# Hybrid decoder layer, one core: decay tables behind the softmax maxima, sample rows by transpositions, one-column row selector, row norm ahead of the attention

## What is computed

```python
h = rms_norm(x, norm_g) * (1 + scale) + shift
proj = h @ w_in                        # D_MODEL 1024 -> 3328 columns
qa, ka, va, za, qb, fb, ib, zb = jnp.split(proj, SPLIT_POINTS, axis=-1)
...                                    # A: QK norm, partial rotary
ya = window_attention(qa, k_all, v_all, pos0, sinks) * jax.nn.silu(za)
...                                    # in it: m = maximum(max(s), sink); p = exp(s - m) / sum
log_f = jnp.log(lbh + (1 - lbh) * jax.nn.sigmoid(zf))     # B: decay f ...
k_in = (1 - lbh) * jax.nn.sigmoid(-zf)                    # ... and key k, from fb
o, s_new = hgrn2_chunked(qb, log_f, k_in, ib, s0)         # S <- f S + k v^T, o = q S
yb = rms_norm(o, o_norm_g) * jax.nn.silu(zb)
g_a, g_b = jnp.split(jax.nn.sigmoid(h @ w_merge + b_merge), 2, axis=-1)
y = g_a * (ya @ w_proj_a) + g_b * (yb @ w_proj_b)
out = x + gate * (y @ w_out)
```

## Time and profile before

| | |
|---|---|
| median of 3 runs | 1617.27 us (1616.54 to 1617.92) |
| profiled execution, its own time | 1617.43 us |
| its span, first to last instruction | 1614.5 us |
| busy shares of the span | PE 97%, PEld 79%, DVE 47%, ACT 34%, POOL 51% |
| chain that ended last | PE 88% |
| HBM traffic | 106 GB/s over the span |

### The profile page before, as it was taken

The page is one execution under the profiler, slowest core; times in us unless marked ns, Lnnn a source line. Parts: engine busy times, 40 slices in busy tenths (PEclk is TensorE's granted clock), DMA queues, the critical chain, the costliest instruction groups (busy, mean ns, idle before and its releaser), DMA issues.

```text
span 1614.5 us, 32929 instructions
## 1 busy us (share of the span) xinstructions
PE 1564.4 (97%) x13608; PEld 1268.2 (79%) x13608; DVE 752.2 (47%) x1930; ACT 555.2 (34%) x1131; POOL 822.6 (51%) x1080
## 2 busy tenths in 40 slices
PE   5999999999999999999999999999999999999998
PEld 2787778877888778888879877788888977788886
DVE  3665554233458655532245665623334655623122
ACT  3334323434322432333422343244432344143330
POOL 2425333556673633455756452437777363337671
PEclk9999999999999999999999999999999999999999
DMA  9723112344565321233365331223455331123351
GB/s 321 230 77 93 54 55 66 92 120 129 170 164 124 102 77 51 70 93 117 92 184 132 85 92 54 67 72 115 137 174 156 86 105 54 55 79 91 93 163 67
DMA packets 304971, 175.87 MB, mean 109 GB/s; under 512 B 74158, under 2 KB 290567, under 8 KB 304808
## 3 DMA queue, kind: packets, MB, share of 16 engines
q1 hardware_dynamic: 304824, 173.79, 37.3%
HBM read 159.69 MB, written 11.96 MB: 106 GB/s over the span
## 4 chain that ended last, share of the span: by engine, by line
PE 88%; DVE 6%; issue 2%; ACT 2%; SPq 2%; DMA 1%; POOL 0%; DVEq 0%
PE ps_D L751 50%; PE ps_D L748 24%; PE ps_XD L806 2%; SPq L503 2%; ACT p_or_hf L1107 1%; PE ps_XB L885 1%; PE ps_XA L918 1%; PE ps_XA L907 1%; PE ps_XB L933 1%; PE ps_XA L938 1%; PE ps_XB L932 1%; DMA th_t<-in_w_ada 1%; DVE p_or_hf L1462 1%; PE ps_XC L818 1%; PE ps_XA L885 1%
## 5 line engine op out<-in xcount | busy, mean ns | idle before, releaser
L1650 POOL TENSOR_TENSOR w_lo_t<-w_raw,w_hi_t 128x256 fp32r<-128x256 f32 x928 | 676.9, 764 | 632.1 <-ACT w_hi_t L964 631.8
L751 PE MATMUL ps_D<-h_hi_t,w_hi_t 128*128 128x512 f32 x1024 | 414.9, 405 | 0.1
L751 PE MATMUL ps_D<-h_hi_t,w_lo_t 128*128 128x512 f32 x1024 | 400.4, 391 | 1.2 <-issue 1.2
L751 PE MATMUL ps_D<-h_lo_t,w_hi_t 128*128 128x512 f32 x1024 | 400.8, 391 | 0.0
L964 ACT ACTIVATE w_hi_t<-w_raw 128x1024 fp32r<-128x1024 f32 x232 | 240.2, 1052 | 78.8 <-PE ps_D L748 45.0
L751 PEld LDWEIGHTS ps_D<-h_hi_t,w_hi_t 128*128 128x128 f32 x1024 | 193.0, 188 | 51.9 <-issue 14.8
L751 PEld LDWEIGHTS ps_D<-h_hi_t,w_lo_t 128*128 128x128 f32 x1024 | 192.8, 188 | 42.0
L751 PEld LDWEIGHTS ps_D<-h_lo_t,w_hi_t 128*128 128x128 f32 x1024 | 193.2, 189 | 36.3 <-issue 0.3
L748 PE MATMUL ps_D<-w_hi_t,h_hi_t 128*128 128x384 f32 (+1 forms) x384 | 141.9, 370 | 3.0 <-issue 1.4
L748 PE MATMUL ps_D<-w_hi_t,h_lo_t 128*128 128x384 f32 (+1 forms) x384 | 136.4, 355 | 1.5 <-issue 1.5
L748 PE MATMUL ps_D<-w_lo_t,h_hi_t 128*128 128x384 f32 (+1 forms) x384 | 136.4, 355 | 0.0
(11 more groups left out here) (390 smaller groups left out, 2373.5 us busy)
## 6 DMA issues: line engine op xcount, KB each, us to landing
w_raw<-in_w_in SPq DMA_DIRECT2D x72, 512.0 KB, 3.9
w_raw<-in_w_merge SPq DMA_DIRECT2D x64, 512.0 KB, 4.0
w_raw<-in_w_in SPq DMA_DIRECT2D x64, 256.0 KB, 3.9
w_raw<-in_w_out SPq DMA_DIRECT2D x32, 512.0 KB, 4.1
x_or_AT<-in_x_prompt SPq DMA_DIRECT2D x20, 512.0 KB, 5.2
w_raw<-in_w_proj_a SPq DMA_DIRECT2D x64, 128.0 KB, 3.0
w_raw<-in_w_proj_b SPq DMA_DIRECT2D x32, 256.0 KB, 3.2
xr<-in_x_prompt SPq DMA_DIRECT2D x16, 512.0 KB, 4.8
```

What stands on the lines that cost most here:

```text
L751: ins = mm(bank[:, :], w[:, s0, k0 + k, :], a[:, k, :], start=go, stop=end)
L1650: ins = g_.tensor_tensor(w_lo[:, c, k:k + 2], w_raw[:, n % NRAW, k:k + 2], f32(w_hi[:, c, k:k + 2]), ALU.subtract)
```

## The change

Five edits:

- DVE's evacuation of units f0, f1 and f3 (their two tables) moves behind the side tasks: f0 and f1 to the end of the second half of their own unit, f3 to the end of the first half of the next unit (`AFTER_SCORES`).
- `sx` transposes the four 128x128 pieces of srow as they are (128 columns each), and DVE then adds the four row groups in a new step, `column_sums`, whose result the tanhs of ACT and the products of DVE read. The bank is now freed by DVE in every case, and in the first pass ACT waits for DVE.
- `vB` is one matmul: the values' high and low parts lie stacked in rows 64 to 71 and 96 to 103 of one tile, with zeros between, and the stationary operand is one column of a small selector, broadcast to 128.
- The large selector's cast at the start of the second pass is gone, a second cast of the values' high part takes its place, and three small instructions that fill the new tiles stand at DVE's start.
- `srms` moves from unit 26 to unit 10 of the second pass and `soss` from unit 28 to unit 11.

```diff
@@ -208,8 +208,8 @@
         for _b in range(NS):
-        put(1, 26, 1, "srms", 0)
-        put(1, 28, 1, "soss", 0, "XC")
+        put(1, 10, 1, "srms", 0)
+        put(1, 11, 1, "soss", 0, "XC")
...
+AFTER_SCORES = {UIX[("f", 0)]: (UIX[("f", 0)], 1), UIX[("f", 1)]: (UIX[("f", 1)], 1), UIX[("f", 3)]: (UIX[("f", 3)] + 1, 0)}
+SUMMED = {a: n + 1 for n, a in enumerate((2, 3, 6, 7, 8, 9, 10))}
...
-        rowsR = sb("rows_r", [8, 1280], F32R)
+        rowsR = sb("rows_r", [104, 1280], F32R)
-        esel = esel_t[0:8, :].rearrange("p (b n) -> p b n", b=NS)
-        ib_hi, ib_lo = rowsR[:, 0:512], rowsR[:, 768:1280]
+        ib_hi, ib2 = rowsR[0:8, 0:512], rowsR[64:104, 0:512]
...
+        esel = sb("esel", [P, NS], F32R)
...
+        red = part(64).rearrange("p (s c b) -> p s c b", s=2, b=NS)
...
                     else:
                         for c in range(nb):
-                            ins = mm(bank[:, NS * c:NS * c + NS], srow[:, P * c:P * c + P], sel[:, 0:NS],
-                                     start=True, stop=True)
+                            ins = tr(bank[:, P * c:P * c + P], srow[:, P * c:P * c + P], ident[:, :])
...
                 elif task == "vB":
                     s.wait_ge("s_ib", 1)
-                    mm(bank[:, :], esel[:, a, :], ib_hi, start=True, stop=False)
-                    ins = mm(bank[:, :], esel[:, a, :], ib_lo, start=False, stop=True)
+                    ins = mm(bank[:, :], esel[64:104, a:a + 1].broadcast_to([40, P]), ib2, start=True, stop=True)
...
                 elif task == "sOT":
-                    s.freed(1, "sx", 4 + a)
+                    s.wait_ge("s_oT", a + 1)
                     for c in range(4):
                         ins = tr(bank[0:NS, P * c:P * c + P], oT[:, 4 * a + c, :], ident[:, :])
...
                 elif task == "sx" and it == 0 and a != 4:
-                    s.full(*key)
-                    src = bank[:, 0:32].rearrange("p (h b) -> p h b", b=NS)
+                    s.freed(*key)
+                    src = red[:, SUMMED[a] % 2]
                     if a == 3:
-                        s.free(fn(thS, src, ACT.Tanh, scale=0.5), *key)
+                        s.done(fn(thS, src, ACT.Tanh, scale=0.5), "s_th")
                     elif a < 7:
                         s.done(fn(tS[:, 0:4] if a == 2 else tS[:, 4:8], src, ACT.Tanh, scale=0.5), "s_th")
                     else:
                         for c in range(4):
                             kind, j = BLOCKS[GROUPS[0][a][c]]
                             cb = 8 * (kind == "gb") + j
-                            ins = fn(thg[:, 2 * j + (kind == "gb"), :], bank[:, NS * c:NS * c + NS], ACT.Tanh, scale=0.5,
+                            ins = fn(thg[:, 2 * j + (kind == "gb"), :], src[:, c, :], ACT.Tanh, scale=0.5,
                                      bias=bm_half[:, cb:cb + 1])
-                        s.free(ins, *key)
+                        s.done(ins, "s_th")
...
             s.done(cp(lmask[:, :, :].rearrange("p l n -> p (l n)"), lm_in))
+            s.done(cp(esel[64:96, :], ident[64:96, 64:72]))
+            s.done(cp(esel[96:104, :], ident[96:104, 96:104]))
+            s.done(ts(ib2[0:32].rearrange("p (n c) -> p n c", c=P), ident[64:96].unsqueeze(1).broadcast_to([32, 4, P]),
+                      0.0, None, ALU.mult))
...
+            def column_sums(it, a, key, dst=None):
+
+                s.full(*key)
+                if dst is None:
+                    n = SUMMED[a]
+                    if n > 2:
+                        s.wait_ge("s_th", n - 2)
+                    dst = red[:, n % 2]
+                if it and a == 0:
+                    s.wait_ge("s_th", SUMMED[10])
+                ins = v.tensor_reduce(dst, bank_of(key)[:, 0:TB].rearrange("p (c g b) -> p c b g", g=4, b=32)[:, :, 0:NS, :],
+                                      AX.X, ALU.add)
+                free(ins, *key)
+
+            def bank_of(key):
+                return pb[BANK[key]]
...
                 elif task == "sx" and it == 0 and a == 3:
-                    s.freed(*key)
+                    column_sums(it, a, key)
+                    s.wait_ge("s_th", SUMMED[a])
                     fw, kw = fs[:, :].unsqueeze(2).broadcast_to([P, HB, NS]), ks[:, :].unsqueeze(2).broadcast_to([P, HB, NS])
                     s.done(tt(fS, thS, fw, ALU.mult))
                     do(tt(kS, thS, kw, ALU.mult))
                     s.done(tt(fS, fS, fb[:, :].unsqueeze(2).broadcast_to([P, HB, NS]), ALU.add))
                     do(tt(kS, kS, kb[:, :].unsqueeze(2).broadcast_to([P, HB, NS]), ALU.add))
                 elif task == "sx" and it == 0 and a == 4:
-                    s.full(*key)
-                    free(cp(qS, bank[:, 0:32].rearrange("p (h b) -> p h b", b=NS)), *key)
+                    column_sums(it, a, key, qS)
                 elif task == "sx" and it == 0 and a in (2, 6):
-                    s.wait_ge("s_th", 1 + (a == 6))
-                    free(stt(zaS if a == 2 else zbS, tS[:, 0:4] if a == 2 else tS[:, 4:8], 1.0,
-                             bank[:, 0:32].rearrange("p (h b) -> p h b", b=NS), ALU.add, ALU.mult), *key)
+                    column_sums(it, a, key)
+                    s.wait_ge("s_th", SUMMED[a])
+                    do(stt(zaS if a == 2 else zbS, tS[:, 0:4] if a == 2 else tS[:, 4:8], 1.0, red[:, SUMMED[a] % 2],
+                           ALU.add, ALU.mult))
+                elif task == "sx" and it == 0:
+                    column_sums(it, a, key)
...
                 elif task == "sx" and it == 1 and a < 4:
-                    s.full(*key)
-                    free(stt(tS[:, 0:4], thg[:, 4 * a:4 * a + 4, :], 1.0, bank[:, 0:32].rearrange("p (c b) -> p c b", b=NS),
-                             ALU.add, ALU.mult), *key)
+                    column_sums(it, a, key, red[:, 0])
+                    s.wait_ge("s_th", SUMMED[10])
+                    do(stt(tS[:, 0:4], thg[:, 4 * a:4 * a + 4, :], 1.0, red[:, 0], ALU.add, ALU.mult))
                     do(tt(hS[:, 2 * a:2 * a + 2, 0:NS], tS[:, 0:4:2, :], tS[:, 1:4:2, :], ALU.add), "s_y")
                 elif task == "sx" and it == 1:
-                    s.full(*key)
                     c = 4 * (a - 4)
-                    free(tt(oT[:, c:c + 4, :], bank[:, 0:32].rearrange("p (c b) -> p c b", b=NS), gate_s[:, c:c + 4, :],
-                            ALU.mult), *key)
+                    column_sums(it, a, key, red[:, 0])
+                    do(tt(oT[:, c:c + 4, :], red[:, 0], gate_s[:, c:c + 4, :], ALU.mult), "s_oT")
...
                     if (it, u) == (1, 0):
                         s.wait_ge("h_lo", h_tiles(0, 3))
                         s.wait_ge("s_win", 32)
-                        do(cp(esel, ident[0:8, 0:8].unsqueeze(2).broadcast_to([8, 8, P])))
                         do(cp(ib_hi, ibS))
-                        do(tt(ib_lo, ibS, f32(ib_hi), ALU.subtract), "s_ib")
+                        s.done(cp(rowsR[64:72, 0:512], ibS))
+                        do(tt(rowsR[96:104, 0:512], ibS, f32(ib_hi), ALU.subtract), "s_ib")
                         do(v.memset(R3[:, :], 0.0))
                         do(cp(qz_b.rearrange("p h b c -> p h (b c)")[:, :, 0:232:33], qS), "esel")
                     for hf_ in (0, 1):
@@ -1631,11 +1652,14 @@
                         early = [x_ for x_ in tasks if hf_ and x_[0] in ("PV", "norm")]
                         for task, a, _, key in early:
                             side(it, task, a, key)
-                        if hf_:
+                        if hf_ and u not in AFTER_SCORES:
                             evac(it, u)
                         for x_ in tasks:
                             if x_ not in early:
                                 side(it, x_[0], x_[1], x_[3])
+                        for n in AFTER_SCORES:
+                            if AFTER_SCORES[n] == (u, hf_):
+                                evac(it, n)
```

More of the change, by code:

```diff
@@ L243 @@
            "lvl", "dgp", "at0", "smax", "p_exp", "p_norm", "kst", "on", "yf", "yh", "yl", "y7f", "y7h", "y7l", "x_in0", "x_in1", "xst", "rstd",
-           "xn", "h_hi", "h_lo", "grow", "s_rows", "s_th", "s_sq8", "s_sc", "s_exp", "s_p", "ckv",
+           "xn", "h_hi", "h_lo", "grow", "s_rows", "s_th", "s_sq8", "s_sc", "s_exp", "s_p", "ckv", "s_oT",
            "s_f", "s_ib", "esel", "s_sq", "s_yb", "s_y", "s_o", "s_o1", "s_win", "s_st_out", "xsr"]
@@ L352, in build @@
         grow = R1[:, 0:D]
-        first = ExitStack()
-        R23 = first.enter_context(nc.sbuf_tensor("p_or_hf", [P, 2048], F32))
-        first.close()
-        esel_t = sb("esel_t", [P, 1024], F32R)
-        sb("upper_half", [P, 1024])
+        R23 = sb("p_or_hf", [P, 2048])
         R2, R3 = R23[:, 0:1024], R23[:, 1024:2048]
@@ L425, in build @@
         smx, ses, ssum = small(4)[0:8], small(4)[0:8], small(4)[0:8]
-        sS = sb("smS", [P, 704])
+        sS = sb("smS", [P, 768])
         def part(n, start=[0]):
```

## The result

| | before | changed |
|---|---|---|
| median, 4 runs each | 1616.9 us (1616.35 to 1617.92) | 1602.97 us (1601.32 to 1604.57) |
| ratio | | 0.9916, 95% interval 0.9904 to 0.9928 |
| profiled execution, own time and span | 1617.43, 1614.5 us | 1604.57, 1602.6 us |

The change makes the kernel 0.84% faster, 13.9 us. The forecast was 1599.5; the time lies in its range, 3.5 us above it.

A forecast was written before the change was run, and what follows sets the result against it. PE, busy 97% of the span, was taken to bound the kernel. Gains of 21.9 us less 4.0 of cost gave 17.9 off 1617.4: 1599.5 us, range 1594 to 1605.

The forecast's parts named there:

- PV 1, passes two to four: Ahead of PV 1, moved tables shorten the wait from 2.98 to 0.9: 2.05 us a pass, 6.1 gained.
- clock behind it: Behind PV 1 in passes two to four, the shorter wait leaves the clock up: 1.5 us a pass, 4.5 gained.
- f3, PV 2: At PV 2's wait of 1.05, moving f3's tables wins 0.4 us in each of three passes: 1.1 gained.
- sx, 13 groups: On PE, four transpositions take 0.41 instead of 0.92 for the products: 13 times 0.5, 6.5 us gained.
- vB: One of two matmuls goes, eight times, 2.6 us; with some lost to waiting at so, 2.0 gained.
- norm out of the scan: At KT, the wait for the scan's last level goes once the row norm leaves DVE there: 1.7 us gained.
- norm ahead of S 1: Second pass: the row norm delays S 1's maxima by 2.06, so PV 0 waits some 2.2: 2.0 us lost.
- first pass, PV 1: Group 3's sums, the wait for tanh and four products ahead of norm make PV 1 later: 0.5 us lost.
- clock at these two: Waits of about 2.0 ahead of second-pass PV 0 and first-pass PV 1: one clock fall charged, 1.5 us lost.
- `norm` starts at 560.5, and PV 1 follows 2.47 later: Second pass, f1's tables behind the maxima: PV 1 comes at 562.9 instead of 565.0, leaving a wait of 0.9.
- srms ... holds DVE to 541.3: Second pass: the row norm begins at 537.16 on DVE, so S 1's maxima come 2.06 later than 539.25.
- rival (i): Row norm or the 2.0 waits cost less, no clock fall, part slack: 3.5 us more gained, 1596; chance 0.12.

The follow-up runs named there:

- the single edit on the kernel before: Kernel before the change, with only the tables of f0 and f1 moved behind norm 2 and norm 3: 1604.9 us, 0.9934.

## Why the prediction was right, and where it was off

The terms, from the starts of the same instructions in the traces of before and of the changed kernel:

| term | forecast | measured |
|---|---|---|
| PV 1, passes two to four | +6.1 | +4.2 (1.40, 1.39, 1.38) |
| clock behind it | +4.5 | +4.5 (1.56, 1.37, 1.56) |
| f3, PV 2 | +1.1 | -1.0 (-0.20, -0.48, -0.28) |
| sx, 13 groups | +6.5 | +6.5 |
| vB | +2.0 | +0.4 |
| norm out of the scan | +1.7 | +2.0 |
| norm ahead of S 1 | -2.0 | -2.8 |
| first pass, PV 1 | -0.5 | -0.9 |
| clock at these two | -1.5 | -3.1 |
| sum | 17.9 | 9.8 |

The span fell by 11.9. The remaining 2.1 are stalls of PE laid to issue (those at `so` left out), 4.6 us in the trace of before and 2.2 in that of after, less 0.3 at the start. The own times of the two profiled executions differ by 12.9, the medians by 13.9; executions of one kernel scatter by more than this 1 us, and a fall of the clock in the first pass, which three of five executions did without, would be enough for it (argued).

That the time fell into the range was in part luck. The nine terms by themselves came to 9.8 of 17.9, which is 1607.6 us and outside it; the fewer stalls laid to issue and the difference between executions, neither of them in the forecast, made up the rest.

**Missing from the forecast: the stalls laid to issue.** All three kernels with products have one of 1.3 to 1.8 near 213 us, none of the eleven with transpositions; summed, the three have 4.6, 4.2 and 2.9 us of them, the eleven 0.6 to 2.2, 1.3 in the mean. Going by the averages (3.9 and 1.3), the transpositions gave some 2.6 us more than their 6.5, which partly made up for what the other terms lacked; only the stall near 213 tells the two groups apart without exception, the rest overlaps with their scatter. PE has 56 matmuls less by them, and what PE's issue waits for there isn't shown.

**Right.** What bounds the kernel, and that a wait of 2.98 costs half as much again in clock where the clock falls behind it: the single edit on the kernel before shows both. The four transpositions at 0.41 beside 0.92, shown by the products put back. By the Trainium skill ("TensorE: Matmul & The Clock Gate", Back-to-back issue gap) that edit should have given nothing (an estimate from its figures for a matmul's spacing); the trace disagrees with it, and agrees with the same page's section on LDWEIGHTS: eight loads or four. The norm's way out of the scan (1.86 with its transposition) and its price ahead of S 1, both shown by putting it back.

**Mis-sized: "`norm` starts at 560.5, and PV 1 follows 2.47 later".** The start was right to 0.15, the 2.47 became 2.97, and a wait of 1.58 stayed instead of 0.9. The sum took `norm`'s steps as they were in the earlier trace rows, and they depend on the moment at which they meet GpSimd. The first of them took 0.16 in 408 of its 448 executions in the 14 traces; in the other 40 it took 0.58 to 0.76, each time with w_lo under way on GpSimd, and each time it ended 0.01 to 0.02 behind the end of a w_lo instruction. The product took 0.82 or 0.83 in the 400 that began while GpSimd did nothing, and 1.03 to 1.40 in the 48 that began beside w_lo. In the earlier trace rows GpSimd was at w_lo too, and the first step met the end of one of its instructions and took 0.16. The Trainium skill ("SBUF — State Buffer", Who interferes with whom) says that an instruction of VectorE with two inputs in SBUF contends with a GpSimd instruction that reads SBUF, and that the one that comes second is blocked until the first has ended; these ends agree with it. No run took w_lo away from `norm` 3, but the row norm, moved to where GpSimd is idle, lost all its slow steps.

**Failed: f3, "only a part is won; I take 0.4 a pass".** The sign was wrong, and the working left out the same thing: that the small instructions ahead of the exponentials would meet w_lo at another moment. (Three times 0.4 is 1.2, not 1.1.) In the third pass two of them took 0.75 and 0.78 instead of 0.18 and 0.15, 1.2 us more in all, and each ended 0.02 behind the end of a w_lo instruction. In the fourth pass of the variant with the row norm where DVE is idle neither was slow: there `norm` 5 starts 4.85 behind S 5 instead of 5.23, the forecast 0.4, and then loses it because its own first step takes 0.59. That the tables end later than ACT needs costs 0.56 (4.85 with them ahead of `norm` 5, 4.29 with them behind it, fourth pass of both), which would have left a gain. Leaving f3's tables in their old place, as in the variant with the tables behind norm, gives 0.47 in the second and in the third pass, shown; in the fourth the waits of this order scatter from 1.10 to 1.94 in seven traces, and nothing is shown. No run set the moment by itself, so what a kernel would need to avoid w_lo there stays open.

**Mis-sized: vB, "one more is likely lost the same way".** The saving was priced at 0.33 for each of eight, and it is 0.24 (0.66 to 0.42), since the matmul that is left holds PE for longer by itself: 1.9, not 2.6. Of it, 1.4 went into waits at two `so`, for DVE's sum of the states (0.20 to 0.45, and 0 to 1.15). I had looked at the wait that stood there before, and not at how little slack the others had. Shown by issuing it twice.

**Mis-sized: "srms ... holds DVE to 541.3" and the clock.** 4.9 instead of 4.15, since three small steps met w_lo, and the transposition, which I laid into the wait, came before the unit's end and cost 0.44 itself. Two falls instead of one. The rival (i), no fall and a hidden norm, is refuted for PV 0: each of the 7 executions with this wait had one.

**Not seen beforehand.** In the first pass the moved tables by themselves delay PV 1 by 0.93, since ACT and the four products of group 3 stood there; the forecast put the whole delay on the sums, which add nothing to it.

## What to carry to other kernels

Work moved off the front of a chain pays only if it leaves the chain: between maxima and `norm` it still stood in the way in part, behind `norm` it didn't. Ask of each moved piece what runs beside it in its new place (a duration read elsewhere may not hold: here small steps of DVE took 0.15 or 0.78 by when they met GpSimd) and where the waiting engine has a true gap; DVE's 5.4 idle us at unit 20 took the norm for 0.2 of PE's time. And where an engine is 97% busy, count its waits singly by length: shortening those above 2 us gives the wait and, mostly, as much again in clock.
